# x's tiles ahead of the parameter rows, far values ahead of the last transposes, k's operands mixed from a difference, and three weight pieces split at other places, in a two-layer decoder kernel

## The reference, cut to what matters

```python
xx = jnp.pad(x, ((0, 0), (1, 0), (0, 0)))[:, :-1] - x
xr, xw, xk, xv, xa, xg = [x + xx * mu[i] for i in range(N_SHIFT_MIX)]
r = xr @ w_r
k = xk @ w_k
v = xv @ w_v
w_log = -jax.nn.softplus(-(w0 + jnp.tanh(xw @ w1) @ w2)) - 0.5
a = jax.nn.sigmoid(a0 + (xa @ a1) @ a2)
g = jax.nn.sigmoid(xg @ g1) @ g2
...
o = jnp.einsum("brnhqk,brnkhd->brnqhd", p / l, vc.astype(jnp.float32))   # three dilations
...
return o.reshape(bsz, seq, ATTN_OUT_WIDTH).astype(xn.dtype) @ w_o
```

## Time and profile before

| | |
|---|---|
| median of three runs | 1462.36 us |
| lowest, highest | 1461.61, 1462.83 us |
| the profiled execution | 1460.64 us |
| its span, first to last instruction | 1458.9 us |
| PE busy | 1332.4 us, 91% |
| DVE busy | 1039.0 us, 71% |
| ACT busy | 859.7 us, 59% |
| POOL busy | 384.8 us, 26% |
| mean granted clock of PE | 0.965 of 2.4 GHz |

### The profile page before, as it was taken

How to read it: one execution, slowest core, us unless ns; L and a number is a source line. 1 busy time by engine, 2 the same in 40 slices (tenths; PEclk the granted TensorE clock), 3 DMA queues, 4 the chain that set the end, 5 groups by cost and what they waited for, 6 DMA issues and landing times. The chain is left out here.

```text
span 1458.9 us, 28563 instructions
## 1 busy us (share of the span) xinstructions
PE 1332.4 (91%) x11003; PEld 1052.9 (72%) x11003; DVE 1039.0 (71%) x1399; ACT 859.7 (59%) x1315; POOL 384.8 (26%) x434
## 2 busy tenths in 40 slices
PE   5999997888899899999995999999998899999993
PEld 3477776777754788888873887878786788888872
DVE  5557854567653799999896527766445899999896
ACT  6735553555522578888883434445544588888782
POOL 1022354276800122233313100011110132223213
PEclk9999999999999999999998999999979999999998
DMA  5322300311474599999993432112131799999984
GB/s 193 116 87 85 117 16 2 94 38 48 141 301 174 203 377 387 384 385 383 382 357 128 145 102 87 59 58 78 68 116 73 248 391 384 391 382 378 380 315 174
DMA packets 160822, 300.11 MB, mean 206 GB/s; under 512 B 17117, under 2 KB 32605, under 8 KB 160720
## 3 DMA queue, kind: packets, MB, share of 16 engines
q1 hardware_dynamic: 149264, 274.01, 52.1%
q0 software_dynamic: 11232, 24.61, 4.7%
q10 hardware_dynamic: 224, 0.07, 0.0%
HBM read 280.35 MB, written 34.60 MB: 216 GB/s over the span
## 5 line engine op out<-in xcount | busy, mean ns | idle before, releaser
L1692 DVE TENSOR_TENSOR moe_wlo<-kept_raw,moe_whi 128x2048 fp32r<-128x2048 f32 x162 | 370.1, 2288 | 41.4 <-ACT moe_whi L1688 36.8
L1688 ACT ACTIVATE moe_whi<-kept_raw 128x2048 fp32r<-128x2048 f32 x192 | 365.0, 1918 | 38.0 <-DMA kept_raw<-in_moe_w_down_dram 15.8
L1699 PE MATMUL all_bank<-moe_whi,moe_xhi 128*128 128x512 f32 x512 | 203.9, 398 | 4.0 <-DVE moe_xlo L1748 4.0
L1701 PE MATMUL all_bank<-moe_whi,moe_xlo 128*128 128x512 f32 x512 | 199.5, 390 | 0.0
L1700 PE MATMUL all_bank<-moe_wlo,moe_xhi 128*128 128x512 f32 x512 | 199.4, 390 | 0.0
L1699 PEld LDWEIGHTS all_bank<-moe_whi,moe_xhi 128*128 128x128 f32 x512 | 96.0, 188 | 26.6 <-issue 4.2
L1701 PEld LDWEIGHTS all_bank<-moe_whi,moe_xlo 128*128 128x128 f32 x512 | 96.1, 188 | 20.8
L1700 PEld LDWEIGHTS all_bank<-moe_wlo,moe_xhi 128*128 128x128 f32 x512 | 96.2, 188 | 18.8
L1699 PE MATMUL all_bank<-moe_whi,moe_hhi 128*128 128x512 f32 x256 | 100.8, 394 | 3.1 <-issue 2.6
L1701 PE MATMUL all_bank<-moe_whi,moe_hlo 128*128 128x512 f32 x256 | 100.4, 392 | 0.0
L1700 PE MATMUL all_bank<-moe_wlo,moe_hhi 128*128 128x512 f32 x256 | 100.3, 392 | 0.0
(11 more groups left out here) (458 smaller groups left out, 2935.1 us busy)
## 6 DMA issues: line engine op xcount, KB each, us to landing
kept_raw<-in_moe_w_gate_dram SPq DMA_DIRECT2D x64, 1024.0 KB, 11.0
kept_raw<-in_moe_w_up_dram SPq DMA_DIRECT2D x64, 1024.0 KB, 12.2
kept_raw<-in_moe_w_down_dram SPq DMA_DIRECT2D x64, 1024.0 KB, 11.2
attn_xhat<-in_w_kv_dram SPq DMA_DIRECT2D x10, 1024.0 KB, 5.1
out_dram<-kept_raw SPq DMA_DIRECT2D x16, 512.0 KB, 4.9
attn_xhat<-in_attn_w_q_dram SPq DMA_DIRECT2D x6, 1024.0 KB, 4.9
all_h<-in_rwkv_w_k_dram SPq DMA_DIRECT2D x4, 1024.0 KB, 9.0
all_h<-in_rwkv_w_v_dram SPq DMA_DIRECT2D x4, 1024.0 KB, 5.1
```

The source lines that it names most:

```text
L1688: nc.scalar.activation(whi[slot % SPLITS][:, :], raw[slot % 6][:, :], ACT.Copy).then_inc(m["hi_ok"], 1)
L1692: nc.vector.tensor_tensor(wlo[slot % SPLITS][:, :], raw[slot % 6][:, :], whi[slot % SPLITS][:, :].bitcast(fp32), ALU.subtract).then_inc(m[ ...
L1699: nc.tensor.matmul(bank[b][:, :], hi[:, k0 + k, :], wh[:, k, :], start=begin and k == 0, stop=False)
L1701: ins = nc.tensor.matmul(bank[b][:, :], lo[:, k0 + k, :], wh[:, k, :], start=False, stop=end and k == 3)
```

## The change

- Start: DVE and PE work on tiles 0 to 2 of x before the parameter block; PE transposes the block ahead of tile 2, into the last quarter of bank 7, and waits for its copy before the last block of tile 2; DVE has its parameter steps ahead of tile 3. `ev_t` becomes two semaphores, and the first mixes wait each for their own block.
- k's x operand: DVE writes the difference of shifted and plain x into `diff` (the storage of `e1`, once `hid` has been computed), four blocks ahead of each half, and mixes with one instruction, x + mu * diff. ACT's part step is gone for q = 0.
- `split_hi(1)` goes ahead of the sixteen sigmoids; `split_hi(10)` ahead of the eight `key_rate`; `split_lo(9)` ahead of key directions 4 to 7; `split_lo(10)` right behind these, ahead of the products of k.
- Attention: PE computes `far_values(0)` ahead of the transposes of the last unit.

```diff
@@ rwkv_project: x_hi, x_lo
-            part(4 * half)
+            if q:
+                part(4 * half)
             for kt in range(4 * half, 4 * half + 4):
-                if kt < 4 * half + 3:
+                if q and kt < 4 * half + 3:
                     part(kt + 1)
...
             def mix(kt):
-                dve.wait_ge(part_ok, KT * q + kt + 1)
+                if q == 0:
+                    dve.wait_ge(diff_ok, kt + 1)
+                    if kt >= 2:
+                        dve.wait_ge(xl_ok, kt - 1)
+                    nc.vector.scalar_tensor_tensor(out=xtemp[:, kt % 2, :], in0=diff[:, kt, :], scalar=mu(ORDER[q], kt),
+                                                   in1=xT[:, kt, 1:T + 1], op0=ALU.mult, op1=ALU.add).then_inc(temp_ok, 1)
+                    return
+                dve.wait_ge(part_ok, KT * (q - 1) + kt + 1)
@@ PE
-            pe.wait_ge(par_in, 16 * 9)
-            nc.tensor.transpose(bank[7][:, 0:P], parrow[:, :], g["ident"][:, :]).then_inc(par_tr, 1)
-            pe.wait_ge(par_ok, 1)
             for j in range(J):
+                if j == J - 2:
+                    pe.wait_ge(par_in, 16 * 9)
+                    nc.tensor.transpose(bank[7][:, P * (J - 1):P * J], parrow[:, :], g["ident"][:, :]).then_inc(par_tr, 1)
                 pe.wait_ge(xhat_ok, j + 1)
                 for kt in range(KT):
+                    if j == J - 2 and kt == KT - 1:
+                        pe.wait_ge(par_ok, 1)
@@ ACT
             act.wait_ge(rest_ok, 1)
-            act.wait_ge(ev_t, KT)
             for name, kt in first_mixes:
+                if name == "g":
+                    act.wait_ge(ev_td if kt % 2 else ev_ta, kt // 2 + 1)
...
             gate(0, 8)
+            split_hi(act, 1)
             for m in range(KT):
...
-            split_hi(act, 1)
             x_hi(act, 0, 1)
...
             x_hi(act, 2, 1)
+            split_hi(act, 10)
             for m in range(KT):
                 key_rate(m)
-            split_hi(act, 10)
@@ DVE
             for j in range(J):
+                if j == J - 1:
+                    dve.wait_ge(par_tr, 1)
+                    V.tensor_copy(par[:, :], bank[7][:, P * (J - 1):P * J]).then_inc(par_ok, 1)
+                    dve.wait_ge(par_ok, 1)
+                    V.tensor_scalar(rest_mu[:, :], par[:, MU:MU + 6 * KT], -1.0, 1.0, ALU.mult, ALU.add).then_inc(rest_ok, 1)
+                    V.tensor_scalar(omk[:, :], par[:, KA_:KA_ + KT], -1.0, 1.0, ALU.mult, ALU.add).then_inc(small, 1)
                 dve.wait_ge(rms, j + 1)
...
+            def differences(lo, hi):
+                dve.wait_ge(unit, start["hid"] + 1)
+                for kt in range(lo, hi):
+                    V.tensor_tensor(diff[:, kt, :], xT[:, kt, 0:T], xT[:, kt, 1:T + 1], ALU.subtract).then_inc(diff_ok, 1)
+
             split_lo(dve, 0)
+            differences(0, 4)
             x_lo(dve, 0, 0)
             gate(0, 8)
+            differences(4, KT)
...
             x_lo(dve, 2, 1)
+            split_lo(dve, 9)
             for m in range(4, KT):
                 key_direction(m)
-            split_lo(dve, 9)
+            split_lo(dve, 10)
...
-            split_lo(dve, 10)
             flush("r", 0, 4)
@@ attention, PE
+            far_values(0)
             transposes(NU - 1)
-            far_values(0)
             far_values(1)
```

More of the change, by code:

```diff
@@ L299, in rwkv_project @@
         rate = xtemp
+        diff = e1
         flat = lambda t: t[:, :, :].rearrange("p a b -> p (a b)")
@@ L319, in rwkv_project @@
         piece_in = [s.sem(f"piece_in{i}") for i in range(2)]
-        part_ok, temp_ok, xh_ok, xl_ok, hi_ok, lo_ok, piece_used = map(s.sem, ["part_ok", "temp_ok", "xh_ok", "xl_ok", "hi_ok", "lo_ok", "piece_used"])
+        part_ok, diff_ok, temp_ok, xh_ok, xl_ok, hi_ok, lo_ok, piece_used = map(s.sem, ["part_ok", "diff_ok", "temp_ok", "xh_ok", "xl_ok", "hi_ok", "lo_ok", "piece_used"])
         sumsq, rms, rstd_ok, xhat_ok, root_in = map(s.sem, ["sumsq", "rms", "rstd_ok", "xhat_ok", "root_in"])
-        par_tr, par_ok, rest_ok, tr, ev_t, zero_ok = map(s.sem, ["par_tr", "par_ok", "rest_ok", "tr", "ev_t", "zero_ok"])
+        par_tr, par_ok, rest_ok, tr, ev_ta, ev_td, zero_ok = map(s.sem, ["par_tr", "par_ok", "rest_ok", "tr", "ev_ta", "ev_td", "zero_ok"])
         started, mixed, unit, ev_act, ev_dve, g_stored, v_stored = map(s.sem, ["started", "mixed", "unit", "ev_act", "ev_dve", "g_stored", "v_stored"])
@@ L487, in begin @@
                 elif u == 0:
-                    pe.wait_ge(ev_t, KT)
+                    pe.wait_ge(ev_ta, KT // 2)
+                    pe.wait_ge(ev_td, KT // 2)
                 return bank[u % 8]
@@ L627, in _ @@
                 act.wait_ge(tr, kt + 1)
-                nc.scalar.activation(xT[:, kt, 1:T + 1], bank[kt][:, :], ACT.Copy, scale=g["par"][:, GMIX + kt:GMIX + kt + 1]).then_inc(ev_t, 1)
+                nc.scalar.activation(xT[:, kt, 1:T + 1], bank[kt][:, :], ACT.Copy, scale=g["par"][:, GMIX + kt:GMIX + kt + 1]).then_inc(ev_ta, 1)
             act.wait_ge(rest_ok, 1)
-            act.wait_ge(ev_t, KT)
             for name, kt in first_mixes:
+                if name == "g":
+                    act.wait_ge(ev_td if kt % 2 else ev_ta, kt // 2 + 1)
                 nc.scalar.activation(mixes[name][:, kt, :], xT[:, kt, 1:T + 1], ACT.Copy, scale=rest(name, kt)).then_inc(started, 1)
@@ L719, in _ @@
             par = g["par"]
-            dve.wait_ge(par_tr, 1)
-            V.tensor_copy(par[:, :], bank[7][:, 0:P]).then_inc(par_ok, 1)
             V.memset(xT[:, :, 0:1], 0.0).then_inc(zero_ok, 1)
             V.memset(reset[:, :], 1.0).then_inc(reset_ok, 1)
-            dve.wait_ge(par_ok, 1)
-            V.tensor_scalar(rest_mu[:, :], par[:, MU:MU + 6 * KT], -1.0, 1.0, ALU.mult, ALU.add).then_inc(rest_ok, 1)
-            V.tensor_scalar(omk[:, :], par[:, KA_:KA_ + KT], -1.0, 1.0, ALU.mult, ALU.add).then_inc(small, 1)
             dve.wait_ge(reset_ok, 1)
@@ L735, in _ @@
                 dve.wait_ge(tr, kt + 1)
-                V.tensor_scalar(xT[:, kt, 1:T + 1], bank[kt][:, :], par[:, GMIX + kt:GMIX + kt + 1], None, ALU.mult).then_inc(ev_t, 1)
+                V.tensor_scalar(xT[:, kt, 1:T + 1], bank[kt][:, :], par[:, GMIX + kt:GMIX + kt + 1], None, ALU.mult).then_inc(ev_td, 1)
             dve.wait_ge(zero_ok, 1)
-            dve.wait_ge(ev_t, KT)
             for i, (name, kt) in enumerate(first_mixes):
+                if name == "g":
+                    dve.wait_ge(ev_td if kt % 2 else ev_ta, kt // 2 + 1)
                 dve.wait_ge(started, i + 1)
```

## The result

The changed kernel takes 1444.81 us (four runs, 1441.94 to 1448.71) against 1462.59 us for the kernel before (four runs beside them, 1461.61 to 1464.59): a ratio of 0.988 with a 95% interval of 0.985 to 0.991, 17.8 us less. That is 7.9 us under the forecast of 1452.7 and 1.7 us under the low end of the range. In later runs the kernel before had a median of 1459.57 us over 63 executions (1453.95 to 1468.43), and the changed kernel, all ten executions together, 1444.92: 14.7 us less. So some 3 us of the miss lie in the three runs that the forecast started from, which were slower than most that followed; the rest is the kernel. The three later batches ran on three different chips, with medians of 1460.48, 1459.90 and 1458.60 us for the kernel before; whether the slower start is the chip or chance was not tested.

The account below looks back on a forecast made before the run. The chain was spread over PE, weight transfers and the experts' splits; in the changed stretches PE's waits counted. Start 4.7, k 3.8, r minus 2.2 and attention 3.4 made 9.7 us gained: 1452.7 us, range 1446.5 to 1458.

Parts of the forecast that it names:

- the step from profile to median: Sum made in the profiled execution's time, 1460.64 us, 1.7 us under the median of 1462.36; difference then taken from the median.
- Attention: End of attention: far_values(0) fills PE's 2.57 us wait, everything behind comes a group sooner; 3.4 us gained, bounds 2.6 and 4.5.
- clock stays up: Rival, attention: far_values and turns take half of their 18 us, bounded by DVE; about 5 us more gained, 1447.7; chance 0.10.
- Start: Start of the kernel: first mix on ACT at 16.6 or 16.7 instead of 21.37; 4.7 us gained, bounds 4.4 and 4.9.
- k: Projection k: piece 1 follows piece 0 without a wait, half the low clock's cost returns; 3.8 us gained, bounds 2.5 and 5.
- Pieces 9 and 10: Weight splits in r: waits of 2.71 and 1.21 go, piece 11 comes late instead; 2.2 us lost, bounds 0.9 and 3.6.
- r: The part of the projections with pieces 9 to 11, forecast to take 2.2 us in the sum.
- Piece 11 isn't late: Rival, r part: products at half of 1.13 us would make it give 5.6 instead of costing 2.2; 1444.9; chance 0.07.
- Given back in the experts: Rival: gains are given back in the experts, where DMA is busy and transfers are on the chain; 1462; chance 0.09.
- DVE and POOL hold each other up: Rival, r part: two holds per product of k, eight taking 16.6 us more, straight onto piece 11; 1469; chance 0.03.

Follow-up runs that it names:

- the four extra matmuls: Kernel before, old order, with four matmuls of unused result put into the wait ahead of attention's last transposes: 1452.97 us, ratio 0.994.
- The mended kernels: Piece 11's split put earlier: on the changed kernel 1437.31 us; on the kernel before, with splits 9 and 10 moved too, 1451.54 us.
- the kernel with one extra matmul: Kernel before with one matmul of unused result put into the wait ahead of attention's last transposes: 1451.89 us, ratio 0.995.

## Why the prediction was wrong, and where it was right

**The sum.** By the spans the forecast was short by 14.7 - 9.7 = 5.0 us. The terms: attention 9.6 instead of 3.4, the projections 6.7 instead of 6.3, the experts +1.0, the chunks -2.5. The other 2.9 us of the 7.9 come from the step from profile to median: I took the profiled execution to lie 1.7 us under it, and that of the changed kernel lies 1.2 us above. With 63 executions of the kernel before up to 14.5 us apart, this step deserved a bound of its own and had none.

**Attention: the step that failed.** The gap was read rightly, and so was the time of the last transposes: 1069.31 is 271.8 us into the stage, where 1073.93 was 271.9 before, since ACT's probabilities set it. What failed is the sentence that the clock would be at 0.50 behind the filled wait. It rested on the earlier trace rows: the groups "held the clock at 0.50 though PE was busy throughout". Rows of a low clock can't tell what the same matmuls do at the high one. They don't raise a clock that has fallen, and they don't lower one that is up: 1.90 us a group in the changed kernel, 3.68 us for two behind the four extra matmuls. From the last transposes to the last `turn` it was 1096.13 - 1073.93 = 22.2 us before and is 1080.79 - 1069.31 = 11.5 us now. The rival "clock stays up" had the mechanism and said 8.4 (3.4 and 5); it counted far values and turns, not the first seven output matmuls, which also ran at half clock behind them (0.43 us apart instead of 0.23). Against it I had held that 0.8 us of idle would be left. It is there (0.84 us), and no profile that has the line moved shows a fall at that place. With 0.10 that rival was priced far too low: what had to be asked was whether the low clock has any cause left once its wait is gone.

DVE's merges did not stay as hidden as I had them, which costs little. They stand back to back from 1074.70 on, where DVE had 1.1 us of idle a group before:

```profile
1076.03 1.07 DVE L2666 TENSOR_TENSOR attn_ol<-all_bank,attn_oh 128x512 fp32r<-128x512 f32 x1
1077.01 0.68 DVE L2658 TENSOR_TENSOR attn_scores<-all_bank,attn_inv 128x512 f32<-128x512 f32 x1
1077.73 0.69 DVE L2662 TENSOR_TENSOR attn_oacc<-attn_scores,attn_oacc 128x512 f32<-128x512 f32 x1
1078.34 1.06 DVE L2666 TENSOR_TENSOR attn_ol<-all_bank,attn_oh 128x512 fp32r<-128x512 f32 x1
```

**Start: right.** 4.9 us against 4.7, at the upper bound of 4.9; alone it gave 4.2 us by the ratio and 4.9 by the medians, and its lead was kept.

**k: the new wait was not priced.** k was to give 3.8 (2.5 to 5) and gives 0.1 to 1.7 against its own removal. Two terms were mis-sized. The copy of `hid` comes 1.46 us later than without the k part (45.24 against 43.78), not 1.1, within its bound of 1.6. But the step behind it had no price: PE waits 1.9 and 3.1 us for this copy in the two profiles (4.5 in the kernel without the moves of pieces 9 and 10) instead of 0.6 to 1.6, and with these waits the clock fell, for 3.4 us in one profile and 6.8 in the other, under g2. That held up ACT's copies of g2 (the 1.93 us of idle above) and the sigmoids, and k began 41.7 and 42.9 us behind the first mix instead of the 61.7 - 21.37 = 40.3 of the forecast (its own terms add up to 61.6). Piece 1 was to come 1.1 us sooner than before and came when it had come before. The gain of the clock behind the old wait is there; it was partly paid back with a fall at a new place.

**Pieces 9 and 10: right in kind, at the low end in size.** The forecast had 2.2 us lost (0.9 to 3.6). Alone the move costs 2.8 us by the ratio (0.7 to 4.8), 1.4 by the medians, and by the profiles 0.2, or 1.0 and 1.2 where the clock had fallen alike; taken out of the changed kernel it makes no difference that the intervals show. The new wait was put at 5 us or more and is 4.4 to 4.5; the low part of piece 11 was to end at 189.5 to 190.5 (198 to 199 less the expected lead of 8.5) and ended at 189.8. The mended kernels show what was hidden behind piece 11: 6.0 us on the kernel before, and 5.8 and 7.4 against the two profiles of the changed kernel, against the forecast's 5.6. That the projections as a whole give 6.7 and 5.0 us in the two profiles, against 6.3, is in part luck: k fell 2 to 4 us short, r cost about 1 us less, and how the clock falls early in the stage moves the net by about a microsecond. ACT's and DVE's chain to piece 11 doesn't absorb what comes before it: `split_hi(10)` waits 3.3 us for PE with the k part and without it.

The split of piece 10 took 2.28 us ahead of POOL's work, not 3.33. The Trainium skill, page "SBUF — State Buffer", in its part on the shared port pair, has VectorE ops with two SBUF inputs and GpSimd ops that read SBUF exclude each other for the whole instruction; this row agrees (POOL's first instruction for a key, begun 0.5 us after the split, took 4.13 us, and the second such one 1.42; the seventh, begun 0.4 us after the split of piece 11, took 3.03), as does a split in the middle of POOL's work in k (3.31 us at 73.04), though the agreement is by durations alone, and the sum didn't turn on it.

**The other rivals.** "Piece 11 isn't late" is refuted in four kernels with a wait of 4.4 to 4.5 us. "Given back in the experts": 325.2 and 331.0 us against 325.7 and 331.5, refuted. "DVE and POOL hold each other up": the eight products ran from 168.04 to 175.98, 1.0 us each instead of 1.13, refuted.

**What stays open.** Which idle stretch takes the clock down is not settled: 0.86 to 0.90 us followed by 0.84 never did in seven profiles, 0.90 followed by 1.71 did in the only one, and perhaps not in other executions, and 2.57 did in all five (each time for 20.5 us). Nor is the chunks' time, 258.5 to 264.9 us in the same code, explained by the microseconds at 0.50 alone: 28.1 of them went with 261.4 us, 25.2 with 264.9.

## What to carry to other kernels

Here a wait of TensorE cost its length and what followed at half clock. Where short matmuls followed, the stage got 9.6 us shorter for a wait of 2.57, and it was not the fault of these matmuls: price the removal of such a wait with the whole tail gone as its own case, and don't give it small odds unless a run of the same matmuls at the high clock speaks against it. When a wait is removed by putting work ahead on another engine, look at the wait that this work pushes back (here `hid` and piece 11) and price its clock too; each of the two was worth more when mended (4 and 6 to 8 us) than the part that had lengthened it. And take the reference time of a kernel whose clock falls at other places from one execution to the next from many executions: three within 1.2 us of each other stood 2.8 us above the median of 63.

## What the runs showed of the hardware that was not expected

The clock can fall after the wait is over: in the kernel with one extra matmul PE was back at work at 1068.94 and the clock fell at about 1070.7, in the middle of matmuls without a gap, and stayed at 0.50 for 17 us with PE busy. Four matmuls whose result nobody reads, 3.6 us long in a wait of 2.57, shortened the stage by 6.5 us. And the same far matmuls run at either level for as long as they last: 0.22 us each in 6.92 us for 32, or 0.12 in 1.90 us for 16.
